# Third attention of a hybrid layer: values with tokens on the partitions, the divisor from a column of ones, normalized along the free axis and turned by transposes

## The chip, the cores and the metric

One core of one Trainium2 chip runs the whole program in one launch. The metric is the time of an execution on the device, in microseconds (us). The engines are named as in the profile: PE (TensorE, with PEld for its weight loads), DVE (VectorE), ACT (ScalarE), POOL (GpSimd) and SP (SyncE, which here starts the weight transfers).

## The reference

The program computes two layers of a hybrid block and then a second block, on 512 tokens with a model width of 1024, all in float32. Only the third branch of the two layers is touched by the change. It is an mLSTM with 4 heads of 128; the kernel computes it as a masked attention over all 512 tokens:

```python
s = einsum('bhtd,bhsd->bhts', q, k) * w_intra        # w_intra: decay of token s as seen from token t
num = einsum('bhts,bhse->bhte', s, v)
den = sum(s, axis=-1)
h = num / maximum(abs(den), exp(-m_row))             # divisor with a floor
# head_layer_norm, over the 128 values of a head
y = (h - mean(h)) * rsqrt(var(h) + 1e-6)
y_c = y * ml_norm_w * sigmoid(ml_o)
branch = y_c * silu(ml_z)                            # then w_branch, gates and w_out
```

With D the divisor of a token, the norm of num/D equals (num - mean(num))/sqrt(var(num) + eps*D^2); the changed kernel uses that form.

## The kernel before

All activations lie transposed: features on the 128 partitions, the 512 tokens along the free axis. Weights are streamed in chunks of 128x1024 float32 by SP into a ring of 4. Each chunk is split into a rounded high part by ACT (`Weights.round`, L120) and a low part by POOL (`Weights.rest`, L147), and a product of a 1024-deep layer takes 8 x 3 matmuls in fp32r over 512 columns (`Weights.product`, L171: high x high, low x high, high x low). Such a product is called dense below; a product of a branch (`gated_product`) is 4 x 3 matmuls. Matmuls that are not split run in true fp32, and the profile shows each of them as two records, one for each pass; a transpose is one record.

The order of the work is written out by hand, and every engine walks through the same list of results (`layer_groups`, L235). A result that takes a bank of the pair `proj` waits until the result two places before it in the list has been emptied (`Groups.open`, L289); six more banks, `att`, hold scores. `Groups.whole` waits for a result, `Groups.empty` signs its bank off, `Groups.moved` waits for that.

The stage of the change stands at the end of each layer's attentions (PE from L968, ACT from L1190, DVE from L1473, POOL from L1576). For each head h, PE computes the dense products `mlo` and `zc` (the two gates of the branch), two branch products `proj2h,0` and `proj2h+1,0` of the first branch, the scores of head h+2 (`ml_scores`, 4 matmuls of 512, 384, 256 and 128 columns) and these three:

- `den`: ones (128x128) as weights against the weighted scores `probs`, 4 matmuls of 512 to 128 columns. It gives the divisor's sum on all 128 partitions.
- `num`: the values `mv` as weights against the same `probs`.
- `var`: ones against the square of the result, one matmul of 512 columns, for the norm.

The values were centred before by DVE (`centre`, L1400, 8 times a layer), so `num` has mean zero over a head. DVE takes the maximum of |den| (ACT, Abs) and the floor, inverts it (L1482), multiplies `num` with it (L1484), and, after ACT has squared and PE has summed, inverts the root (L1490) and applies weight, root and both gates (L1491 to L1494). Before the divisor of the next head it empties the banks of the branch products (`first_gated`, L1457) and weighs the next head's scores (`ml_weigh`, L1463). The floor exp(-m) is one row a head; POOL writes it to memory and spreads it over the partitions by DMA (`spread_row`, L1544), as it does with the row for the decay. ACT computes the decay factors (`ml_decay`, L1175), and POOL sets the upper triangles to zero (L1580). The same stage follows again for the second layer. Behind it come the other branch products with their gates (`GATES`), in which the third branch is read from `zc`.

Of the kernel before, what the change touches and what calls it, by code (L numbers as in the profile page):

```python
# [7 lines left out]
F32 = mybir.dt.float32  # L8
F32R = mybir.dt.float32r
ALU = mybir.AluOpType  # L10
# [12 lines left out]
IDX_H = 4  # L23
TOPK = 128
# [3 lines left out]
TAKEN = -3e38  # L28
ALIVE = -2.5e38
# [200 lines left out]
AFTER_SUMS = [["gate00"], ["gate30"], ["gate40"], ["gate70"]]  # L230
GATES = [(0, 1), (1, 1), (0, 2), (1, 2)] + [(d, k) for d in range(2, KD) for k in (1, 2)]
# [3 lines left out]
def layer_groups(l):  # L235
# [22 lines left out]
    for i, (d, k) in enumerate(GATES):  # L258
        g += [(f"gate{d}{k}", "a")] + ([(f"var{ML_H - 1}", "a")] if i == 0 else []) + [(f"proj{d}{k}", "v")]
# [284 lines left out]
def hybrid_layers(nc, stack, S, A, scratch):  # L544
# [31 lines left out]
    dv_at, dv = here(nc), sb("dv", [P, TB, T])  # L576
# [13 lines left out]
    acol = sb("acol", [P, TB, ML_H])  # L590
# [33 lines left out]
    mq, mk, mv = dq, dk, dv  # L624
# [3 lines left out]
    hml, dn, hsq = bias[:, 0:T], bias[:, T:2 * T], misc[:]  # L628
    spread_mu, spread_floor = [idx[:, i, :] for i in range(2)], [idx[:, 2 + i, :] for i in range(2)]
# [27 lines left out]
    s_fl = [sem(f"s_floor_spread{i}", 32) for i in range(2)]  # L657
    s_decay = sem("s_decay", 4 * ML_H)
    s_masked = sem("s_masked", 3)
    s_csq = sem("s_csq", 1)  # L660
# [19 lines left out]
    s_centred = sem("s_centred", 8)  # L680
    s_silu = sem("s_silu", 2)
    s_gate0 = sem("s_gate0", 1)
# [4 lines left out]
    s_sq2 = sem("s_sq2", 4)  # L687
    s_mlz = sem("s_mlz", 4)
# [52 lines left out]
    def tensor(pe, l):  # L741
# [71 lines left out]
        for b in range(TB):  # L813
            tr = pe.transpose(out[:, b * ML_H:(b + 1) * ML_H], g_a[:, b * P:(b + 1) * P], ident[0:ML_H, 0:ML_H])
# [147 lines left out]
        def ml_var(h):  # L962

            out = G.open(pe, f"var{h}")
            pe.wait_ge(s_sq2.sem, s_sq2.base + h + 1)
            G.close(pe.matmul(out[:, :], ones, hsq, start=True, stop=True))

        for h in range(ML_H):  # L968
            dense(f"mlo{h}")
            if h >= 1:  # L970
                ml_var(h - 1)
            dense(f"zc{h}")
            if h == 0:
                ml_scores(0)
                ml_scores(1)
            gated_product(2 * h, 0)
            pe.wait_ge(s_ws.sem, s_ws.base + 3 * (h + 1))
            for n in ("den", "num"):
                out = G.open(pe, f"{n}{h}")
                if h == 0 and n == "num":  # L980
                    pe.wait_ge(s_centred.sem, s_centred.base + 2 * TB)
                for s in range(TB):
                    w = ones if n == "den" else mv[:, s, h * P:(h + 1) * P]
                    mm = pe.matmul(out[:, s * P:T], w, probs[:, h % 2, KOFF[s]:KOFF[s] + WK[s]],  # L984
                                   start=(s == 0), stop=(s == TB - 1), skip_group_check=True)
                G.close(mm)
            if h + 2 < ML_H:
                ml_scores(h + 2)
            gated_product(2 * h + 1, 0)

        for i, (d, k) in enumerate(GATES):
# [2222 lines left out]
```

## Time and profile before

| quantity | value |
|---|---|
| three timed runs | 2600.92, 2596.46, 2601.33 us; median 2600.92 |
| span of the profiled execution (first to last instruction) | 2593.4 us |
| the profiled execution's own time | no figure apart from its span; the timed runs lie 3.1 to 7.9 us above the span |
| PE busy | 2523.2 us (97%) |
| DVE, ACT, POOL busy | 1097.1, 1062.5, 1303.8 us (42, 41, 50%) |
| granted clock of TensorE | 0.993 of full speed |
| DMA | 227.23 MB, mean 88 GB/s |

The busy share of PE counts overlapping records once, and the duration of a matmul record holds its passage through the array as well. What a matmul costs in a stream is therefore read from the distance between the starts of two records and not from their durations. The stage of the change lies at 388 to 484 us in the first layer and at about 1073 to 1170 us in the second.

### The profile page before, as it was taken

Reading aid. Unit: us, or ns where it says so; the run is one execution under the profiler, and the core shown is the slowest. Engines: PE = TensorE matmul, PEld = TensorE weight load, DVE = VectorE, ACT = ScalarE, POOL = GpSimd, SP = SyncE. Lnnn points to the kernel's source line nnn. Section 1 sums busy time; section 2 is a strip of 40 time slices with the busy share of each in tenths; the row PEclk is TensorE's granted clock in tenths of the full one; section 3 lists DMA queues with packets and bytes.
Section 4 is the critical chain, followed back from the end, with each engine's and each line's share of the span. In section 5 each row is a group of like instructions: output and inputs, shape, how many; then the busy total and the mean of one; then the engine's idle time right before and its main releaser. Section 6 shows DMA issues by size and latency. Waiting matters only on the chain.

```text
span 2593.4 us, 32107 instructions
## 1 busy us (share of the span) xinstructions
PE 2523.2 (97%) x12502; PEld 2033.3 (78%) x12502; DVE 1097.1 (42%) x1893; ACT 1062.5 (41%) x1605; POOL 1303.8 (50%) x1790
## 2 busy tenths in 40 slices
PE   8999999999999999999999999999989899999998
PEld 6777887788777788778888888877967688888886
DVE  5855635522485563552243113098355422311101
ACT  5334667423433466732343323242355323322321
POOL 5444655555544465545555554574433255555453
PEclk9999999999999999999999999999999999999999
DMA  4222122222222212222232222331221122222222
GB/s 153 86 90 82 66 65 82 73 98 98 90 82 67 81 66 66 81 74 97 95 109 95 95 95 97 105 131 66 82 74 66 41 98 98 90 98 98 98 98 81
DMA packets 63698, 227.23 MB, mean 88 GB/s; under 512 B 7431, under 2 KB 8967, under 8 KB 63420
## 3 DMA queue, kind: packets, MB, share of 16 engines
q1 hardware_dynamic: 61276, 217.28, 24.9%
q0 software_dynamic: 2272, 7.90, 1.1%
q8 instruction: 100, 1.64, 0.3%
q14 instruction: 50, 0.41, 0.1%
HBM read 222.98 MB, written 4.01 MB: 88 GB/s over the span
## 4 chain that ended last, share of the span: by engine, by line
PE 89%; DVE 7%; ACT 3%; issue 1%; DMA 1%; DVEq 0%; SPq 0%; ACTq 0%
PE proj L180 75%; PE proj L877 1%; PE att L180 1%; PE att L914 1%; PE proj L984 1%; ACT b_logits L2371 1%; PE att L856 1%; PE att L900 1%; DVE h_low L530 1%; PE att L867 1%; PE att L958 1%; PE att L2029 1%; DVE hT L536 1%; DVE rstd L1490 1%; PE proj L763 0%
## 5 line engine op out<-in xcount | busy, mean ns | idle before, releaser
L157 POOL TENSOR_TENSOR weight_low<-ring,weight_high 128x256 fp32r<-128x256 f32 x1592 | 1229.2, 804 | 1145.7 <-ACT weight_high L127 1124.3
L180 PE MATMUL proj<-h_high,weight_high 128*128 128x512 f32 x2016 | 796.5, 395 | 17.9 <-ACT b_big L2214 13.0
L180 PE MATMUL proj<-h_high,weight_low 128*128 128x512 f32 x2016 | 786.0, 390 | 0.0
L180 PE MATMUL proj<-h_low,weight_high 128*128 128x512 f32 x2016 | 785.2, 389 | 0.0
L127 ACT ACTIVATE weight_high<-ring 128x1024 fp32r<-128x1024 f32 x393 | 413.9, 1054 | 410.4 <-PE proj L180 378.9
L180 PEld LDWEIGHTS proj<-h_high,weight_high 128*128 128x128 f32 x2016 | 378.8, 188 | 130.6 <-ACT b_big L2214 14.3
L180 PEld LDWEIGHTS proj<-h_low,weight_high 128*128 128x128 f32 x2016 | 378.9, 188 | 80.2
L180 PEld LDWEIGHTS proj<-h_high,weight_low 128*128 128x128 f32 x2016 | 379.3, 188 | 75.5 <-issue 0.2
L2562 DVE TENSOR_TENSOR b_big<-proj,b_big 128x512 f32<-128x512 f32 x42 | 29.0, 691 | 376.3 <-PE proj L180 376.3
L180 PE MATMUL proj<-b_act_high,weight_high 128*128 128x512 f32 x352 | 137.2, 390 | 0.0
L180 PE MATMUL proj<-b_act_high,weight_low 128*128 128x512 f32 x352 | 136.9, 389 | 0.0
L180 PE MATMUL proj<-b_act_low,weight_high 128*128 128x512 f32 x352 | 136.9, 389 | 0.0
L2214 ACT ACTIVATE b_big<-proj 128x512 f32<-128x512 f32 x58 | 34.6, 597 | 198.2 <-PE proj L180 198.1
L2583 DVE SCALAR_TENSOR_TENSOR xT<-proj,xT 128x512 f32<-128x512 f32 x16 | 11.1, 691 | 198.1 <-PE proj L180 198.1
L1507 DVE TENSOR_TENSOR turned<-proj,probs 128x512 f32<-128x512 f32 x32 | 22.1, 692 | 165.4 <-PE proj L180 165.3
L180 PE MATMUL proj<-weight_high,h_high 128*128 128x256 f32 x288 | 82.6, 287 | 2.1 <-ACT sv L1009 2.1
L180 PE MATMUL proj<-weight_low,h_high 128*128 128x256 f32 x288 | 81.5, 283 | 0.0
L180 PE MATMUL proj<-weight_high,h_low 128*128 128x256 f32 x288 | 81.5, 283 | 0.0
L180 PE MATMUL proj<-z_high,weight_high 128*128 128x512 f32 x192 | 76.2, 397 | 2.2 <-DVE turned L1507 2.2
L180 PEld LDWEIGHTS proj<-b_act_high,weight_high 128*128 128x128 f32 x352 | 66.1, 188 | 13.8 <-issue 0.2
L180 PEld LDWEIGHTS proj<-b_act_high,weight_low 128*128 128x128 f32 x352 | 66.1, 188 | 13.8
L180 PEld LDWEIGHTS proj<-b_act_low,weight_high 128*128 128x128 f32 x352 | 66.1, 188 | 13.7
(473 smaller groups left out, 3735.1 us busy)
## 6 DMA issues: line engine op xcount, KB each, us to landing
ring<-in_stream SPq DMA_DIRECT2D x398, 512.0 KB, 3.3
idx<-gate_rows POOLq DMA_DIRECT2D x16, 256.0 KB, 4.6
xT<-in_x SPq DMA_DIRECT2D x4, 512.0 KB, 6.5
out<-hT SPq DMA_DIRECT2D x4, 512.0 KB, 2.7
bias_rows<-bias_row SPq DMA_DIRECT2D x2, 512.0 KB
b_logits<-in_mem POOLq DMA_DIRECT2D x1, 1024.0 KB, 6.3
consts<-in_const SPq DMA_DIRECT2D x1, 832.0 KB, 10.3
bias_rows<-bias_row SPq DMA_DIRECT2D x1, 768.0 KB
```

The lines of the kernel that those rows point to most:

```text
L127: self.s_high.on(act.activation(self.high[:, c % HIGH, :], self.raw[:, c % self.slots, :], ACT.Copy))
L157: self.s_low.on(pool.tensor_tensor(self.low[:, c % self.slots, cols], self.raw[:, c % self.slots, cols], self.high[:, c % HIGH, cols], ALU ...
L180: mm = pe.matmul(out, a, b, start=(k == 0 and i == 0), stop=(k == n - 1 and i == 2))
L530: S.s_hl.on(dve.tensor_tensor(S.h_low[:, k, :], S.hT[:, k, :], S.h_high[:, k, :], ALU.subtract))
L536: S.s_h.on(dve.scalar_tensor_tensor(out[:, k, :], S.xT[:, k, :], weights[:, k:k + 1], S.att[5][:, :], ALU.mult, ALU.mult))
L856: mm = pe.matmul(att[2 * bank + hh][:, col:col + WQ[b]], dq[rows(hh), p, b * P:(b + 1) * P], dk[rows(hh), p, 0:WQ[b]], start=True, stop=True)
L867: tr = pe.transpose(att[2 * bank + hh][:, col + (b - s) * P:col + (b - s + 1) * P], probs[:, hh, OQ[b] + s * P:OQ[b] + (s + 1) * P], ident)
L877: mm = pe.matmul(out[rows(hh), s * P:T], v[:, s, h * HD:(h + 1) * HD], turned[:, hh, KOFF[s]:KOFF[s] + WK[s]], start=(s == 0), stop=(s == ...
L900: mm = pe.matmul(att[3 * hh + bank][:, col:col + WK[s]], sk[rows(hh), p, s * P:(s + 1) * P], sq_[rows(hh), p, s * P:T], start=(s != 3), st ...
L914: mm = pe.matmul(att[3 * hh + bank][:, col + (u - s) * P:col + WK[s]], signs[:, 0:P] if u == s else signs[:, P:2 * P], x, start=False, sto ...
L2214: G.empty(act.activation(out, bank[:, :] if src is None else src(bank), func, **kw), name)
L2562: G.empty(dve.tensor_tensor(big[:, i, :], bank[:, :], big[:, i, :], ALU.mult), f"{n}b{i}")
```

## The change

The scores stay as they are. The values are no longer centred; they are stored 130 apart for each head, with two columns of ones behind the 128 values. `num` now takes the 128x128 blocks of `probs` as weights and 129 columns of `mv` (128 values and a one) as the moving operand: 10 matmuls a head for the lower triangle of blocks, written to two of the head's three `att` banks (`s_num` signs it off). Tokens then stand on the partitions and the divisor's sum is column 128. `den` and `var` are gone, and with them their banks. DVE computes divisor, mean and variance in `ml_stats` with bn_stats and bn_aggr, ACT takes a root of 128x4 numbers (`ml_root`), DVE inverts it and applies mean and factor (`ml_apply`) into `by_token`, PE turns the result with four transposes a head into a `proj` bank (`y`), and DVE multiplies it with weight and gates (`ml_gated`; `ml_gate` forms the product of the gates beforehand). The floor is transposed along with the decay's column (`at`: 8 instead of 4 small transposes), and its exponential is taken of 128x16 numbers. The four DMAs a layer that spread the floor are gone. The order of the third stage is written out anew (`THIRD`), and with it the order on ACT, DVE and POOL. The sigmoid over `mixed` on ACT is split in two. The z_high parts of the third branch are taken at the first two of the later gates (two each) instead of all at the second.

```diff
+THIRD = [["mlo0", "zc0", "mls0", "mls1", "proj00", "num0", "proj10"],
+         ["mlo1", "y0", "mls2", "num1", "zc1", "proj20", "y1", "mls3", "proj30"],
+         ["num2", "mlo2", "zc2", "proj40", "y2", "proj50"],
+         ["num3", "mlo3", "zc3", "proj60", "y3", "proj70"]]
...
@@ -253,10 +259,9 @@
     for p in range(PAIRS_H):
         g += [(n, "a") for n in BEFORE_SUMS[p] + AFTER_SUMS[p]] + [(f"sb{p}", "v")]
     for h in range(ML_H):
-        g += [(f"mlo{h}", "a")] + ([(f"var{h - 1}", "a")] if h else []) + [(f"zc{h}", "a"), (f"proj{2 * h}0", "v")]
-        g += [(f"den{h}", "a"), (f"num{h}", "v"), (f"proj{2 * h + 1}0", "v")]
...
+        g += [(n, "v" if n[0] in "py" else "a") for n in THIRD[h] if n[:3] not in ("num", "mls")]
+    for d, k in GATES:
+        g += [(f"gate{d}{k}", "a"), (f"proj{d}{k}", "v")]
     g += [(f"out{d}", "v") for d in range(KD)]
     return g
...
@@ -621,12 +628,17 @@
     mix_low = rounded("mix_low", [P, KD, T], mix_at)
     mix_high2 = [rounded(f"mix_high{i}", [P, 4, T], at) for i, at in enumerate((sq_at, sv_at))]
     mix_high = [mix_high2[k // 4][:, k % 4, :] for k in range(KD)]
-    mq, mk, mv = dq, dk, dv
+    dv = dv_all[:, 0:TB * T].rearrange("p (a b) -> p a b", a=TB)
+    mv = dv_all[:].rearrange("p (a b c) -> p a b c", a=TB, b=ML_H)
+    mq, mk = dq, dk
     ckv = idx[:, 3, :]
     gate = probs[:].rearrange("p a b -> p (a b)")[:, 0:3 * T].rearrange("p (a b) -> p a b", a=3)
     part = turned[:].rearrange("p a b -> p (a b)")[:, 0:2 * T].rearrange("p (a b) -> p a b", a=2)
-    hml, dn, hsq = bias[:, 0:T], bias[:, T:2 * T], misc[:]
-    spread_mu, spread_floor = [idx[:, i, :] for i in range(2)], [idx[:, 2 + i, :] for i in range(2)]
+    by_token = [bias[:, i * T:(i + 1) * T].rearrange("p (a b) -> p a b", a=TB) for i in range(2)]
+    spread_mu = [idx[:, i, :] for i in range(2)]
+    stats = small[:, 0:6 * TB].rearrange("p (a b) -> p a b", a=TB)
+    moments = small[:, 24:24 + 2 * TB].rearrange("p (a b) -> p a b", a=TB)
+    s_den, s_square, s_dev, s_factor = (small[:, 32 + TB * i:32 + TB * (i + 1)] for i in range(4))
     csq = dk[:, 0, :]
     tflat = turned[:].rearrange("p a b -> p (a b)")
...
@@ -810,8 +823,10 @@
         dense("zb1")
         out = G.open(pe, "at")
         pe.wait_ge(s_gates.sem, s_gates.base + 1)
-        for b in range(TB):
-            tr = pe.transpose(out[:, b * ML_H:(b + 1) * ML_H], g_a[:, b * P:(b + 1) * P], ident[0:ML_H, 0:ML_H])
+        for i, rows_ in enumerate((g_a, g_m)):
+            for b in range(TB):
+                at = (i * TB + b) * ML_H
+                tr = pe.transpose(out[:, at:at + ML_H], rows_[:, b * P:(b + 1) * P], ident[0:ML_H, 0:ML_H])
         G.close(tr)
         dense("zb2")
         dense("zb3")
...
@@ -952,46 +967,50 @@
                 pe.wait_ge(s_a_exp.sem, s_a_exp.base + 3 * HEADS)
                 pe.wait_ge(s_silu.sem, s_silu.base + 2)
             else:
-                pe.wait_ge(s_ws.sem, s_ws.base + 3 * (h - 1))
+                pe.wait_ge(s_by_token.sem, s_by_token.base + h - 1)
             for s in range(TB):
                 bank, col = KPLACE[s]
                 mm = pe.matmul(att[3 * (h % 2) + bank][:, col:col + WK[s]], mk[:, h, s * P:(s + 1) * P], mq[:, h, s * P:T],
                                start=True, stop=True)
             s_K.on(mm)
-        def ml_var(h):
-
...
+        def ml_values(h):
+            pe.wait_ge(s_ws.sem, s_ws.base + 3 * (h + 1))
+            if h == 0:
+                pe.wait_ge(s_ones.sem, s_ones.base + 1)
+                G.moved(pe, "mlv7")
+            for b in range(TB):
+                out, col = att[3 * (h % 2) + b // 2], VALUE * (b % 2)
+                for s in range(b + 1):
+                    at = KOFF[s] + (b - s) * P
+                    mm = pe.matmul(out[:, col:col + ML_D + 1], probs[:, h % 2, at:at + P], mv[:, s, h, 0:ML_D + 1],
+                                   start=(s == 0), stop=(s == b), skip_group_check=True)
+            s_num.on(mm)
+        def ml_turn(h):
+            out = G.open(pe, f"y{h}")
+            pe.wait_ge(s_by_token.sem, s_by_token.base + h + 1)
+            for b in range(TB):
+                tr = pe.transpose(out[:, b * P:(b + 1) * P], by_token[h % 2][:, b, :], ident)
+            G.close(tr)
         for h in range(ML_H):
-            dense(f"mlo{h}")
-            if h >= 1:
...
+            for n in THIRD[h]:
+                if n[:3] == "mls":
+                    ml_scores(int(n[3:]))
+                elif n[:3] == "num":
+                    ml_values(int(n[3:]))
+                elif n[0] == "y":
+                    ml_turn(int(n[1:]))
+                elif n[:4] == "proj":
+                    gated_product(int(n[4]), 0)
+                else:
+                    dense(n)
+        for d, k in GATES:
             dense(f"gate{d}{k}")
-            if i == 0:
-                ml_var(ML_H - 1)
             gated_product(d, k)
         for d in range(KD):
             out = G.open(pe, f"out{d}")
...
         def fill(names):
             for n in names:
                 if n[:3] in ("sbv", "mlv"):
                     i = int(n[3:])
-                    move(n, (sv if n[0] == "s" else mv)[:, i % TB, (i // TB) * HALF:(i // TB + 1) * HALF],
-                         rows_=slice(0, HALF))
+                    if n[0] == "s":
+                        move(n, sv[:, i % TB, (i // TB) * HALF:(i // TB + 1) * HALF], rows_=slice(0, HALF))
+                        continue
+                    W.round(act, n)
+                    bank = G.whole(act, n)[:, 0:HALF].rearrange("p (a b) -> p a b", a=2)
+                    G.empty(act.activation(mv[:, i % TB, 2 * (i // TB):2 * (i // TB) + 2, 0:ML_D], bank, ACT.Copy), n)
                 elif n[:2] == "ml":
                     h = int(n[3:]) + (4 if n[2] == "k" else 0)
                     if h == 0:
...
@@ -1183,45 +1206,50 @@
                 s_decay.on(act.activation(turned[:, h % 2, KOFF[s]:KOFF[s] + WK[s]], spread_mu[h % 2][:, s * P:T], ACT.Exp,
                                           bias=acol[:, s, h:h + 1]))
-        def ml_var(h):
-
-            move(f"var{h}", rstd[:], ACT.Sqrt, scale=1.0 / ML_D, bias=S.eps)
+        def ml_root(h):
+            act.wait_ge(s_dev2.sem, s_dev2.base + h + 1)
+            s_root.on(act.activation(s_dev, s_dev, ACT.Sqrt))
         ml_decay(0)
+        ml_decay(1)
         move("mlo0", mlo[:, 0, :], ACT.Sigmoid)
         G.moved(act, f"dsa{PAIRS_H - 1}")
         for j in range(4):
             s_zh.on(act.activation(z_high[0][:, j, :], za[:, j, :], ACT.Copy))
         settle(act, s_a)
-        s_gate0.on(act.activation(mixed, mixed, ACT.Sigmoid))
-        for h in range(ML_H):
...
+        s_gate0.on(act.activation(mixed[:, 0:2, :], mixed[:, 0:2, :], ACT.Sigmoid))
+        s_gate0.on(act.activation(mixed[:, 2:KD, :], mixed[:, 2:KD, :], ACT.Sigmoid))
+        move("zc0", zc[:, 0, :], ACT.Silu)
+        W.round(act, "proj00")
+        ml_root(0)
+        W.round(act, "proj10")
+        move("mlo1", mlo[:, 1, :], ACT.Sigmoid)
+        ml_decay(2)
+        ml_root(1)
+        move("zc1", zc[:, 1, :], ACT.Silu)
+        W.round(act, "proj20")
+        ml_decay(3)
+        W.round(act, "proj30")
+        act.wait_ge(s_K.sem, s_K.base + ML_H)
+        G.moved(act, f"sb{PAIRS_H - 1}")
+        for j in range(4):
+            s_zh.on(act.activation(z_high[1][:, j, :], zb[:, j, :], ACT.Copy))
+        for h in (2, 3):
+            ml_root(h)
+            move(f"mlo{h}", mlo[:, h, :], ACT.Sigmoid)
             move(f"zc{h}", zc[:, h, :], ACT.Silu)
             W.round(act, f"proj{2 * h}0")
-            if h + 1 < ML_H:
-                ml_decay(h + 1)
-            move(f"den{h}", dn, ACT.Abs)
             W.round(act, f"proj{2 * h + 1}0")
-            G.moved(act, f"num{h}")
-            s_sq2.on(act.activation(hsq, hml, ACT.Square))
...
+        act.wait_ge(s_num.sem, s_num.base + ML_H)
         for n, (d, k) in enumerate(GATES):
             if n >= 3:
                 G.moved(act, "proj{}{}".format(*GATES[n - 3]))
             move(f"gate{d}{k}", gate[:, n % 3, :], ACT.Sigmoid)
-            if n == 0:
-                ml_var(ML_H - 1)
             W.round(act, f"proj{d}{k}")
-            if (d, k) == (1, 1):
-                act.wait_ge(s_mlz.sem, s_mlz.base + ML_H)
-                for j in range(4):
+            if n < 2:
+                for j in range(2 * n, 2 * n + 2):
+                    G.moved(act, f"y{j}")
                     s_zh.on(act.activation(z_high[2][:, j, :], zc[:, j, :], ACT.Copy))
             if n >= 3 and GATES[n - 1][1] == 2:
                 e = GATES[n - 1][0]
...
@@ -1437,6 +1456,9 @@
         for p in range(PAIRS_H):
             if p == 0:
                 gated(f"dsa{PAIRS_H - 1}", PAIRS_H - 1, za)
+                s_ones.on(dve.memset(mv[:, :, :, ML_D:VALUE], 1.0))
+                dve.wait_ge(s_floor.sem, s_floor.base + 1)
+                link(dve.tensor_scalar(fcol, fcol, FLOOR_TOP, None, ALU.min))
             else:
                 gated(f"sb{p - 1}", p - 1, zb)
             soft_sum(p, 0)
...
         def first_gated(d):
             bank = G.whole(dve, f"proj{d}0")
-            if d == 0:
-                dve.wait_ge(s_gate0.sem, s_gate0.base + 1)
+            dve.wait_ge(s_gate0.sem, s_gate0.base + (1 if d < 2 else 2))
             G.empty(dve.tensor_tensor(mixed[:, d, :], bank[:, :], mixed[:, d, :], ALU.mult), f"proj{d}0")
         def ml_weigh(h):
...
@@ -1465,34 +1484,87 @@
             dve.wait_ge(s_w8m.sem, s_w8m.base + TB * (h + 1))
             dve.wait_ge(s_K.sem, s_K.base + h + 1)
             if h >= 2:
-                G.whole(dve, f"num{h - 2}")
+                dve.wait_ge(s_num.sem, s_num.base + h - 1)
             for bank, n, at in BANKS:
                 s_ws.on(dve.scalar_tensor_tensor(probs[:, h % 2, at:at + n], att[3 * (h % 2) + bank][:, 0:n], ML_D ** -0.5,
                                                  turned[:, h % 2, at:at + n], ALU.mult, ALU.mult))
+        def ml_stats(h):
+            dve.wait_ge(s_num.sem, s_num.base + h + 1)
+            banks = [att[3 * (h % 2) + i][:, 0:2 * VALUE].rearrange("p (a b) -> p a b", a=2) for i in range(2)]
+            for i in range(2):
+                s_vc.on(dve.tensor_tensor(s_den[:, 2 * i:2 * i + 2], banks[i][:, :, ML_D], fcol[:, 2 * i:2 * i + 2, h],
+                                          ALU.max))
+            for b in range(TB):
+                s_vc.on(dve.bn_stats(stats[:, b, :], banks[b // 2][:, b % 2, 0:ML_D]))
+            settle(dve, s_vc)
+            for i in range(2):
+                s_vc.on(dve.scalar_tensor_tensor(s_den[:, 2 * i:2 * i + 2], banks[i][:, :, ML_D], -1.0,
+                                                 s_den[:, 2 * i:2 * i + 2], ALU.mult, ALU.max))
+            settle(dve, s_vc)
+            s_vc.on(dve.tensor_tensor(s_square, s_den, s_den, ALU.mult))
+            for b in range(TB):
+                s_vc.on(dve.bn_aggr(moments[:, b, :], stats[:, b, :]))
+            settle(dve, s_vc)
+            s_dev2.on(dve.scalar_tensor_tensor(s_dev, s_square, EPS, moments[:, :, 1], ALU.mult, ALU.add))
+        def ml_apply(h):
+            dve.wait_ge(s_root.sem, s_root.base + h + 1)
+            link(dve.reciprocal(s_factor, s_dev))
+            if h >= 2:
+                G.whole(dve, f"y{h - 2}")
+            for b in range(TB):
+                x = att[3 * (h % 2) + b // 2][:, VALUE * (b % 2):VALUE * (b % 2) + ML_D]
+                ins = dve.tensor_scalar(by_token[h % 2][:, b, :], x, moments[:, b, 0:1], s_factor[:, b:b + 1],
+                                        ALU.subtract, ALU.mult)
+                if b < TB - 1:
+                    s_vc.on(ins)
+            s_by_token.on(ins)
+        def ml_gate(h):
+            G.moved(dve, f"mlo{h}")
+            G.moved(dve, f"zc{h}")
+            link(dve.tensor_tensor(zc[:, h, :], zc[:, h, :], mlo[:, h, :], ALU.mult))
+        def ml_gated(h):
+            bank = G.whole(dve, f"y{h}")
+            ins = dve.scalar_tensor_tensor(zc[:, h, :], bank[:, :], vecs[:, 41 + h:42 + h], zc[:, h, :], ALU.mult, ALU.mult)
+            G.empty(ins, f"y{h}")
         branch_low(0)
         ml_weigh(0)
-        for h in range(ML_H):
-            if h == 2:
...
+        first_gated(0)
+        ml_weigh(1)
+        ml_stats(0)
+        ml_apply(0)
+        first_gated(1)
+        ml_gate(0)
+        ml_gated(0)
+        ml_stats(1)
+        ml_weigh(2)
+        ml_apply(1)
+        first_gated(2)
+        ml_gate(1)
+        ml_gated(1)
+        first_gated(3)
+        ml_weigh(3)
+        ml_stats(2)
+        branch_low(1)
+        ml_apply(2)
+        first_gated(4)
+        ml_gate(2)
+        ml_gated(2)
+        first_gated(5)
+        ml_stats(3)
+        ml_apply(3)
+        first_gated(6)
+        ml_gate(3)
+        ml_gated(3)
+        first_gated(7)
         def mixed_low(d):
             dve.wait_ge(s_mh.sem, s_mh.base + d + 1)
...
@@ -1570,20 +1642,14 @@
                 for s in range(TB):
                     s_am.on(triangle(turned[:, hh, KOFF[s]:KOFF[s] + P], ALU.is_gt, 1, 0.0))
             W.rest(pool, AFTER_SUMS[p][-1])
-        pool.wait_ge(s_tri.sem, s_tri.base + HEADS)
-        spread_row(1, 0)
-        spread_row(1, 1)
         for h in range(ML_H):
-            W.rest(pool, f"zc{h - 1}" if h else "gate70")
+            W.rest(pool, ("gate70", "gate70", "mlo1", "zc1")[h])
             pool.wait_ge(s_decay.sem, s_decay.base + TB * (h + 1))
             for s in range(TB):
                 s_w8m.on(triangle(turned[:, h % 2, KOFF[s]:KOFF[s] + P], ALU.is_ge, 1, 0.0))
             if h + 2 < ML_H:
-                spread_row(0, h + 2)
-            if 1 <= h < 3:
...
+                spread_row(h + 2)
+        W.rest(pool, "proj30")
         W.rest(pool, f"out{KD - 1}")
     def loads(sp, l):
```

## Rows read from the trace of the kernel before

**Rows 1.** The page: busy time by engine, and the chain that ended last.

```profile
PE 2523.2 (97%) x12502; PEld 2033.3 (78%) x12502; DVE 1097.1 (42%) x1893; ACT 1062.5 (41%) x1605; POOL 1303.8 (50%) x1790
...
PE 89%; DVE 7%; ACT 3%; issue 1%; DMA 1%; DVEq 0%; SPq 0%; ACTq 0%
```

**Rows 2.** Waits of the tensor engine: engine, line, total us, times, longest.

```profile
PE proj L984 <- DVE raw L1461: 6.3, 2, 3.1
...
PE proj L180 <- DVE turned L1507: 2.2, 2, 1.1
...
PE proj L180 <- DVE bias L1484: 1.0, 2, 0.6
```

**Rows 3.** Timeline of PE in third attention, layer 0: start, duration, engine, line.

```profile
403.69 2.40 PE L984 MATMUL proj<-probs,consts_all 128*128 128x512 f32 x8
...
425.13 0.39 PE L180 MATMUL proj<-z_high,weight_high 128*128 128x512 f32 x1
...
427.85 2.32 PE L984 MATMUL proj<-probs,consts_all 128*128 128x512 f32 x8
430.00 2.32 PE L984 MATMUL proj<-probs,dv 128*128 128x512 f32 x8
432.16 2.32 PE L958 MATMUL att<-dq,dk 128*128 128x512 f32 x8
```

**Rows 4.** Timeline of PE around the variance product of head 0.

```profile
418.71 1.02 PE L966 MATMUL proj<-misc,consts_all 128*128 128x512 f32 x2
419.56 0.50 PE L180 MATMUL proj<-h_high,weight_high 128*128 128x512 f32 x1
419.89 0.40 PE L180 MATMUL proj<-h_high,weight_low 128*128 128x512 f32 x1
```

**Rows 5.** Timeline of PE around twenty transposes of the first attention.

```profile
194.89 2.35 PE L867 MATMUL att<-consts_all,probs 128*128 128x128 f32 x20
...
197.31 0.39 PE L180 MATMUL proj<-h_high,weight_low 128*128 128x512 f32 x1
```

**Rows 6.** Timeline of PE: four true fp32 products of 128 columns, eight passes.

```profile
21.67 1.05 PE L503 MATMUL att<-consts_all,scal 128*128 128x128 f32 x8
...
22.80 0.39 PE L180 MATMUL att<-lead_high,weight_low 128*128 128x512 f32 x1
```

**Rows 7.** Line 503 grouped: weight loads, ns min/median/max.

```profile
L503 PEld LDWEIGHTS att<-consts_all,scal x48: 187/190/338, 21.4 to 2584.3; 128*128 128x128 f32 x48
```

**Rows 8.** Timeline of PE and DVE at the longest wait of head 2.

```profile
452.40 4.06 DVE L1455 TENSOR_TENSOR z_low<-zb,z_high 128x512 fp32r<-128x512 f32 x4
...
457.12 2.42 PE L984 MATMUL proj<-probs,dv 128*128 128x512 f32 x8 [3.15 <-DVE raw L1461]
```

**Rows 9.** Timeline of ACT at the head of the stage.

```profile
390.32 1.92 ACT L1183 ACTIVATE turned<-idx,acol 128x512 f32<-128x512 f32 x4
...
397.09 3.60 ACT L1196 ACTIVATE raw<-raw 128x4096 f32<-128x4096 f32 x1
...
402.95 0.60 ACT L1009 ACTIVATE sk<-proj 128x512 f32<-128x512 f32 x1
```

**Rows 10.** Timeline of DVE: small operations, and the weighting of scores.

```profile
256.18 0.17 DVE L1364 TENSOR_SCALAR small<-small 128x4 f32<-128x4 f32 x1
...
257.09 1.28 DVE L1373 TENSOR_SCALAR probs<-probs,small 128x128 f32<-128x128 f32 x4
...
322.92 0.42 DVE L1405 TENSOR_REDUCE small<-dv 128x2 f32<-128x256 f32 x1
```

**Rows 11.** Timeline of DVE in third attention.

```profile
399.01 1.62 DVE L1470 SCALAR_TENSOR_TENSOR probs<-att,turned 128x512 f32<-128x512 f32 x3
...
408.96 3.35 DVE L1482 RECIPROCAL bias<-bias 128x512 f32<-128x512 f32 x1
```

**Rows 12.** Timeline of PE at the gate transposes.

```profile
111.87 0.41 PE L814 MATMUL proj<-consts_all,idx 4*128 4x4 f32 x4
112.62 0.50 PE L180 MATMUL proj<-h_high,weight_high 128*128 128x512 f32 x1 [0.35 <-ACT zb L1009]
```

More of the change, by code:

```diff
@@ L23 @@
 IDX_H = 4
+VALUE = ML_D + 2
 TOPK = 128
@@ L28 @@
 TAKEN = -3e38
+FLOOR_TOP = 1e18
 ALIVE = -2.5e38
@@ L575, in hybrid_layers @@
     dk_at, dk = here(nc), sb("dk", [P, 4, T])
-    dv_at, dv = here(nc), sb("dv", [P, TB, T])
+    dv_at, dv_all = here(nc), sb("dv", [P, TB * ML_H * VALUE])
+    sb("line_up2", [P, LINE_UP])
     sq_at, sq_ = here(nc), sb("sq_", [P, 4, T])
@@ L656, in hybrid_layers @@
     s_mu = [sem(f"s_mu_spread{i}", 32) for i in range(2)]
-    s_fl = [sem(f"s_floor_spread{i}", 32) for i in range(2)]
     s_decay = sem("s_decay", 4 * ML_H)
     s_masked = sem("s_masked", 3)
+    s_ones = sem("s_ones", 1)
+    s_num = sem("s_num", ML_H)
+    s_dev2 = sem("s_dev_square", ML_H)
+    s_root = sem("s_dev_root", ML_H)
+    s_by_token = sem("s_by_token", ML_H)
     s_csq = sem("s_csq", 1)
@@ L960, in ml_scores @@
             s_K.on(mm)
-        def ml_var(h):
-            out = G.open(pe, f"var{h}")
-            pe.wait_ge(s_sq2.sem, s_sq2.base + h + 1)
-            G.close(pe.matmul(out[:, :], ones, hsq, start=True, stop=True))
-        for h in range(ML_H):
-            dense(f"mlo{h}")
-            if h >= 1:
[L971 to L989, printed above, removed]
@@ L1084, in scalar @@
         act.preload_act_table_set("natural_log_exp_and_others")
-        act.wait_ge(s_gates.sem, s_gates.base + 1)
-        s_floor.on(act.activation(g_m, g_m, ACT.Exp))
+        G.moved(act, "at")
+        s_floor.on(act.activation(fcol, fcol, ACT.Exp))
         def fill(names):
@@ L1218, in scalar @@
             move(f"gate{d}{k}", gate[:, n % 3, :], ACT.Sigmoid)
-            if n == 0:
-                ml_var(ML_H - 1)
             W.round(act, f"proj{d}{k}")
-            if (d, k) == (1, 1):
-                act.wait_ge(s_mlz.sem, s_mlz.base + ML_H)
-                for j in range(4):
+            if n < 2:
+                for j in range(2 * n, 2 * n + 2):
+                    G.moved(act, f"y{j}")
                     s_zh.on(act.activation(z_high[2][:, j, :], zc[:, j, :], ACT.Copy))
@@ L1447, in vector @@
                 conv(h)
-            for i in ([], range(4), [], range(4, 8))[p]:
-                centre(i)
         gated(f"sb{PAIRS_H - 1}", PAIRS_H - 1, zb)
@@ L1473, in vector @@
+        def ml_gate(h):
[6 more added lines that the diff above has]
+            G.empty(ins, f"y{h}")
         branch_low(0)
         ml_weigh(0)
-        for h in range(ML_H):
-            if h == 2:
-                branch_low(1)
-            first_gated(2 * h)
-            G.moved(dve, f"den{h}")
-            dve.wait_ge(s_fl[h % 2].sem, s_fl[h % 2].base + 16 * (h // 2 + 1))
-            link(dve.tensor_tensor(dn, dn, spread_floor[h % 2], ALU.max))
-            link(dve.reciprocal(dn, dn))
-            bank = G.whole(dve, f"num{h}")
-            G.empty(dve.tensor_tensor(hml, bank[:, :], dn, ALU.mult), f"num{h}")
-            first_gated(2 * h + 1)
-            if h + 1 < ML_H:
-                ml_weigh(h + 1)
-            settle(dve, s_v)
-            G.moved(dve, f"var{h}")
-            link(dve.reciprocal(rstd[:], rstd[:]))
-            link(dve.scalar_tensor_tensor(hml, hml, vecs[:, 41 + h:42 + h], rstd[:], ALU.mult, ALU.mult))
-            link(dve.tensor_tensor(hml, hml, mlo[:, h, :], ALU.mult))
-            G.moved(dve, f"zc{h}")
-            s_mlz.on(dve.tensor_tensor(zc[:, h, :], zc[:, h, :], hml, ALU.mult))
-            settle(dve, s_mlz)
@@ L1555, in gpsimd @@
                 pool.wait_ge(s_rows_out.sem, s_rows_out.base + 16)
[L1556 to L1557 removed]
+                G.moved(pool, "at")
+                spread_row(0)
+                spread_row(1)
         for p in range(PAIRS_H):
```

46 lines of the change are left out of this document (10 added, 36 removed).

## The prediction

> **What bounds the kernel now.** I read the page first, then the waits of PE, then timelines of the stage that changes. On the page the reader is to see that PE is busy 97% of the span and carries 89% of the chain that ended last [rows 1]; nothing else is near half of either. So an edit is worth what it takes from PE's stream or from PE's waits, and work on DVE, ACT and POOL is worth nothing until it makes PE wait. The table of waits [rows 2] holds three lines that belong to the changed stage: `num` waiting for a bank that DVE frees with a branch product (6.3 us in two waits, one a layer), a product waiting for the gate multiplication (2.2), one waiting for the bank of `num` (1.0). The timeline says why the longest exists: DVE spends 4.06 us on the low parts of the second branch, behind the norm of head 1, and only then empties the bank; PE stands still for 3.15 us [rows 8].
>
> **How the prices are read.** Twelve split matmuls of 512 columns run from 425.13 to 427.85, that is 0.227 us each [rows 3]. Behind a run of true fp32 the first of them takes 0.33 instead (419.56 to 419.89) [rows 4]; I call the 0.10 an edge.
>
> **What goes from PE.** `den` runs from 427.85 to 430.00: 2.15 us. `num` after it takes 2.16 (to 432.16) [rows 3]. `var` with its edge: 419.89 - 418.71 - 0.23 = 0.95 [rows 4]. Removed per head 2.15 + 0.95 = 3.10.
>
> **What comes to PE.** Four transposes a head. Twenty take 197.31 - 194.89 - 0.23 = 2.19 with an edge, so 0.105 each [rows 5]; four are 0.42, with an edge 0.52.
>
> **What changes shape.** `num` was 1280 columns under 4 weight loads; it becomes 10 x 129 = 1290 columns under 10, each in two passes, so 20 loads of 128 columns with only 129 columns to hide one. The trace has no such group with real scores as weights. The old `num` gives 2.16 / 2560 = 0.84 ns a column and pass, so 2.18 us. The nearest row in shape are four fp32 products of 128 x 128: 22.80 - 21.67 - 0.23 - 0.10 = 0.80 for eight passes, 0.10 each, 2.0 for twenty [rows 6]. From above: a load's own record lasts 0.190 us [rows 7]; if that set the pace, twenty passes would be 3.8. I take 2.18: rows 6 have the same loads at almost the same width, at a pace of 0.10. That is +0.02 a head.
>
> Per head 3.10 - 0.52 - 0.02 = 2.56 us, and eight heads (4 in each of 2 layers) give 20.5. The new order also puts y0 next to scores and `num1`, and y1 next to scores, so there are 8 runs of fp32 in a layer where there were 9: 0.2 more over two layers. Sum of PE work: 20.7 us.
>
> The Trainium skill (TensorE: Matmul & The Clock Gate, Part 3: Packing small matmuls) speaks against this: it says that a weight load overlaps a running matmul only where the row groups differ, and all matmuls here use all rows. The transposes of rows 5 load 128 columns for each 128 that they stream and keep 0.105 us, so this trace does not agree. What the rule would make of the time is the third rival below.
>
> **What goes of the waits.** In the new order DVE does the low parts of the second branch behind the statistics of head 2, with two dense products and one branch product of PE still ahead of the next thing needed, and `num` takes no bank of the pair. The 3.35 us reciprocals of 512 columns [rows 11] shrink to 4 columns (0.17, as the small operation in rows 10), so the gates at the end of the stage find their banks empty. I count all three lines: 6.3 + 2.2 + 1.0 = 9.5 us. Their bounds are 0 (another wait stands there) and 9.5.
>
> **What is late next.** I walked PE through the new order with a dense product of 425.13 - 419.56 = 5.57, a branch product of 2.72 and scores of about 2.1 [rows 3, 4]. DVE's chain for one head is ten operations on at most 4 columns at 0.17, four bn_stats that I price by the 256-wide reduction at 0.42, the inverse at 0.17 and four applications at 1.28 [rows 10]: 1.7 + 1.7 + 0.2 + 1.3 = 4.9, and some 0.2 for ACT's root between. The trace shows no bn_stats; from below they are 0.17 each, which takes 1 us off.
> - Head 0: `num0` ends at 403.69 + 2.18 = 405.9, DVE is done at 411.0. PE has a branch and a dense product to do and asks for it at 414.2. Slack 3.
> - Head 1: PE does a dense and a branch product after `num1`, 8.3 us; DVE has the chain and the weighting of head 2, 1.62 [rows 11], between: 6.7. Slack 1.6, the tightest.
> - Head 2: 13.9 us of PE against the chain, the weighting of head 3 and 4.06 of low parts: 10.8. Slack 3. Head 3: 13.9 against 5.1.
> Behind the waiting turn stands all of PE, so each microsecond beyond the slack is lost in full.
>
> At the head of the stage ACT now does the decay of head 1 before emptying `mlo0`: 1.92 us, and the sigmoid over `mixed` (3.60) in two pieces, some 0.2 more [rows 9]. Everything behind slides by 2.1: the bank of `zc0` is empty at 402.95 + 0.60 + 2.1 = 405.65, and PE asks for it at 405.87, after `num0`. That is a margin of 0.2, so between nothing and 0.5 us a layer; I take 0.1. The weighting of head 0 ends at 399.01 + 1.62 = 400.63 [rows 11] and slides to 402.7, a microsecond before `num0` wants it at 403.69 [rows 3].
>
> **At nothing.** Four more small transposes: the four of before take 0.41, and behind them PE waits 0.35 for a bank [rows 12], which covers them but for 0.1. The centring is DVE work in a stage where DVE holds nobody up; the ones and the clamp of the floor go into an idle microsecond there. The floor's DMAs and POOL's issue of them free POOL a little, which is off the path. Copying the values to a stride of 130 moves as many elements as before.
>
> **Sum.** 20.7 + 9.5 - 0.2 = 30.0 us. On the profiled span 2593.4 becomes 2563.4. The span lies 7.5 below the median of the timed runs (2600.92), and I keep that distance: 2570.9.
>
> **The rivals.**
> 1. *The sums hold*, waits gone, no new one above 1 us: 2567 to 2575. 68%. Another 5% for less than 2567, if the block products run at the 0.10 of rows 6 (8 x 0.18 = 1.4 us) and the median before was high; the lowest run was 4.5 below it.
> 2. *The loads set the pace of the block products*: 20 x (0.190 - 0.108) = 1.6 a head, 13 us in all, 2584. For it: 188 to 190 ns is what every load's record shows. Against: rows 5 and 6, whose passes follow each other faster. 8%.
> 3. *The loads hide under nothing*: 20 x 0.190 = 3.8 a head for `num` and 0.76 for the turn, 36.5 in all, 2607. Against it the same rows. 2%. It is what the rule of the Trainium skill (TensorE: Matmul & The Clock Gate, Part 3) would do here.
> 4. *DVE's chain takes the place of the bank waits.* Place: y1 first, then y0 and y2. With 4 us more on each head the stalls are 2.4 + 1 + 1 a layer, 9 in both: 2580. The scalars are many small dependent operations that read PSUM, which speaks for it; the durations of 0.17 speak against. 14% for 2576 to 2590.
> 5. *The same chain, so long that the kernel is slower.* The gain of 30 is lost when both layers wait 15 each: 4x - (3 + 1.6 + 3 + 8.8) = 15, x = 7.9 us more on every head, the chain 13 instead of 5. Even bn_stats at the pace of the reciprocal (6.5 ns a column, rows 11) add only 1.6. 3% for 2606 or more.
>
> **The numbers.** The likeliest case gives 2570.9. The range 2564 to 2585 takes in the first two cases and most of the fourth, the reach of the block products' price (2.0 to 3.8) and of the waits (0 to 9.5 would be 2580). A measurement of this kernel can tell 0.2% (5 us) from no change. Faster by more than that: everything but the third and fifth case and a thin part of the fourth, 95%; within it 1%; slower 4%.
>
> **What would show it.** Right: no records of `var` and `den`; twenty records of 129 columns following each other at 0.105 to 0.11 us; four transposes a head in 0.42; the three lines of rows 2 gone; PE's busy time down by about 20. Wrong: PE standing before a transpose for `by_token` (case 4), or the weight loads of `num` end to end (case 2, 3). The forecast falls if the starts of the block products lie 0.19 apart, or if any wait of the new stage exceeds 2 us.

## The result: 37 us faster, 7 us more than predicted

Four executions of each kernel have medians of 2561.78 us (changed) and 2599.02 us (before): 37.2 us less, ratio 0.9856 with a 95% interval of 0.9841 to 0.9872. The forecast was 2570.9, the range 2564 to 2585: the direction was right, the gain of 30.0 too small, and the time lies 2.2 us below the range.

The page of the changed kernel, its head and its chain, beside [rows 1]: PE is 24.1 us less busy and carries 2 points more of the chain.

```profile
span 2560.3 us, 32269 instructions
...
PE 2499.1 (98%) x12558; PEld 2030.3 (79%) x12558; DVE 1036.3 (40%) x1977; ACT 1043.9 (41%) x1587; POOL 1290.1 (50%) x1782
...
PE 91%; DVE 5%; ACT 3%; DMA 1%; issue 1%; SPq 0%; DVEq 0%; ACTq 0%
```

The waits of PE. The three lines of [rows 2] are gone; one of 0.35 us a time has come, at the branch products behind the turns of heads 2 and 3.

```profile
PE proj L182 <- DVE raw L1480: 1.4, 4, 0.3
```

The timeline of PE: the block products of head 0 and what follows, then turn, scores and block products of head 1. It answers to [rows 3 to 5].

```profile
405.65 2.40 PE L987 MATMUL att<-dv,probs 128*128 128x129 f32 x20
407.80 0.47 PE L182 MATMUL proj<-z_high,weight_high 128*128 128x512 f32 x1
...
416.09 0.60 PE L996 MATMUL proj<-consts_all,bias 128*128 128x128 f32 x4
416.53 2.32 PE L973 MATMUL att<-dq,dk 128*128 128x512 f32 x8
418.69 2.40 PE L987 MATMUL att<-dv,probs 128*128 128x129 f32 x20
420.84 0.47 PE L182 MATMUL proj<-h_high,weight_high 128*128 128x512 f32 x1
```

Twenty passes take 2.15 us from start to start (I had 2.18), the turn 0.44. DVE's chain for head 0, beside [rows 10]:

```profile
408.08 0.23 DVE L1497 TENSOR_TENSOR small<-att,acol 128x2 f32<-128x2 f32 x2
408.23 0.88 DVE L1500 BATCH_NORM_STATS2 small<-att 128x6 f32<-128x128 f32 x4
...
409.82 0.37 DVE L1508 BATCH_NORM_AGGREGATE small<-small 128x2 f32<-128x6 f32 x4
...
410.86 0.18 DVE L1515 RECIPROCAL small<-small 128x4 f32<-128x4 f32 x1 [0.27 <-ACT small L1212]
411.07 1.37 DVE L1520 TENSOR_SCALAR bias<-att,small 128x128 f32<-128x128 f32 x4
```

From 408.08 to 412.44 it takes 4.4 us where I had 5.1, and its result lies there 3.6 us before PE turns it at 416.09.

The stage as a whole, from the first product on the scores of head 0 to the first product behind the last changed wait (the third of the later gates), by the starts of these rows. The kernel before (den of head 0; beyond [rows 3]), layer 0 and layer 1:

```profile
503.66 0.39 PE L180 MATMUL proj<-h_high,weight_high 128*128 128x512 f32 x1
...
1051.41 2.39 PE L984 MATMUL proj<-probs,consts_all 128*128 128x512 f32 x8
...
1152.82 0.39 PE L180 MATMUL proj<-h_high,weight_high 128*128 128x512 f32 x1
```

The changed kernel, the same places (the first one is 405.65 above):

```profile
490.14 0.39 PE L182 MATMUL proj<-h_high,weight_high 128*128 128x512 f32 x1
...
1037.87 2.40 PE L987 MATMUL att<-dv,probs 128*128 128x129 f32 x20
...
1122.37 0.39 PE L182 MATMUL proj<-h_high,weight_high 128*128 128x512 f32 x1
```

Before: 503.66 - 403.69 = 99.97 and 1152.82 - 1051.41 = 101.41. After: 84.49 and 84.50. So the stage gives 15.48 and 16.91 us. The difference between the layers is 1.4 us, and the stretches say where it lies. The kernel before, 4 us of PE behind the wait of head 2, in layer 0 and layer 1. The columns are length, PE busy (records), granted clock as a share of full speed, DMA share and GB/s:

```profile
457.00:461.00 4.00, 3.88 (x15) 1.00 0.00 0
1105.00:1109.00 4.00, 4.00 (x11) 0.65 0.00 0
```

In layer 1 the clock stands at its lower level, 1.2 GHz instead of 2.4, behind the wait. At full clock the change is thus worth 2 x 15.5 = 31.0 us, against the 30.0 of my sum. What the experiments had to find is the rest of the 37.

### The profile page after: what moved, and what is told of

Its sections match the earlier page's. It is cut to its first block, busy times and chain, and to the rows that moved or that the text cites. A ratio compares the mean times of both kernels' runs of the same rounds, so it can differ in the third digit from the quotient of the medians.

```text
span 2560.3 us, 32269 instructions
## 1 busy us (share of the span) xinstructions
PE 2499.1 (98%) x12558; PEld 2030.3 (79%) x12558; DVE 1036.3 (40%) x1977; ACT 1043.9 (41%) x1587; POOL 1290.1 (50%) x1782
## 4 chain that ended last, share of the span: by engine, by line
PE 91%; DVE 5%; ACT 3%; DMA 1%; issue 1%; SPq 0%; DVEq 0%; ACTq 0%
PE proj L182 77%; PE att L182 1%; PE proj L892 1%; PE att L929 1%; ACT b_logits L2437 1%; PE att L871 1%; PE att L915 1%; PE att L987 1%; DVE h_low L535 1%; PE att L882 1%; PE att L973 1%; PE att L2095 1%; DVE hT L541 1%; PE proj L776 0%; PE att L2230 0%
```

## The experiments

Theory A: a wait of PE costs what the trace records. Theory B: the changed kernel is granted more clock as such. Theory C, formed on the repeated trace of the kernel before (e1): a long wait also drops the granted clock to half for some microseconds behind it. Times are medians, of 9 to 15 executions for the kernel before (2597.3 to 2597.7) and of only 4 to 6 for the others. "Over the changed kernel" is against 2561.75, its median in e2 and e10.

How far a median can be trusted, the traces say. Behind the stage of layer 1 the program is the same in every version, and yet it takes from 1433.2 us (e5) to 1443.9 us (e9) there. So single executions can lie up to 11 us apart for reasons outside the changed stage, and the distances between rows of the stage tell more than a median of four.

**e1, the kernel before against itself.** No edit.

> The kernel before, once more against itself, to see how far single executions of one program lie apart and whether its granted clock differs from that of the changed kernel. Theory A (the trace of the change holds: 31.0 us from PE's stream and waits, the rest of the 37.2 us between the medians is chance in the granted clock): ratio 1.000 within 0.002, executions spread over 5 us or more, and their clocks over 0.002. Rival B (the changed kernel is granted more clock as such): the clocks of this one lie below those of the changed kernel on the same chip by 0.002 or more in the mean.

Ratio 0.9999 (0.999 to 1.0007); 2592.01 to 2600.55. The eleven clocks are 0.990 to 0.993, 0.9919 in the mean; four of the changed kernel 0.992 to 0.996, 0.9933 in the mean (e2). That is 0.0013 apart where B asked for 0.002; over 45 executions of the kernel before and 12 of the changed one it is 0.002. So the changed kernel does run at a little more clock, and the trace names a place where the kernel before loses some: the same two waits, in layer 0 and layer 1.

```profile
457.00:461.00 4.00, 3.60 (x6) 0.57 0.00 0
...
1106.00:1110.00 4.00, 3.36 (x5) 0.50 0.02 4
```

`num` of head 2 in layer 0 takes 3.81 us from start to start (457.40 to 461.21), against 2.18 in the first trace (457.12 to 459.30).

```profile
457.40 4.05 PE L984 MATMUL proj<-probs,dv 128*128 128x512 f32 x8 [3.15 <-DVE raw L1461]
461.21 0.48 PE L180 MATMUL proj<-z_high,weight_high 128*128 128x512 f32 x1
```

**e2 and e10, the changed kernel again.** No edit.

> The changed kernel, once more. Theory A: on more executions the difference to the kernel before comes towards the 31 us of the traces, 29 to 34 us, ratio 0.987 to 0.989. Rival B (a clock gain comes on top): it stays at 36 to 38 us, ratio 0.9855 to 0.986, and the mean clock is above that of the kernel before by 0.002.

> The changed kernel a third time, to narrow the difference between the medians. Theory C says: 31.0 us of PE work and waits as the traces give it, and 1.5 to 4.4 us of half clock behind the waits of head 2 (as in the two traces of the kernel before), so 32.5 to 35.5 us faster than the kernel before. Theory A: 31.

2561.73 and 2561.75, ratios 0.9860 (0.9843 to 0.9877) and 0.9858 (0.9843 to 0.9872): 35.8 us both times. Theory A's 31 lies outside both intervals (31.9 and 33.2 us at the least), and C's upper end of 35.5 is inside them, just short of the value.

The traces agree with C more closely. The four spans of the kernel before (the first, e1, e11, e12) have a mean of 2595.6 us, the three of the changed kernel (the first, e2, e10) one of 2561.4: 34.2 us. The two stages alone, read as above in the same seven traces, differ by 34.4 us.

**e3, the order alone.** On the kernel before:

```diff
         for h in range(ML_H):
-            if h == 2:
-                branch_low(1)
             first_gated(2 * h)
...
                 ml_weigh(h + 1)
+            if h == 2:
+                branch_low(1)
             settle(dve, s_v)
```

> The kernel before with one edit: DVE does the low parts of the second branch in the idle time ahead of the norm of head 2 and not before its first branch product. Nothing else of the change is in it. My term for the longest wait says that both waits of 3.15 us go and nothing takes their place: 6.3 us faster, ratio 0.9976. Rival: num waits for the bank anyway, since DVE's chain for the divisor (0.7 + 3.35 + 0.7 us) stands between the branch product and the emptying of num; then under 3 us are won.

9.7 us faster (ratio 0.9965, 0.9953 to 0.9978, which is 5.7 to 12.2 us), where 6.3 were expected. Yet its trace gives back less than 6.3: a small wait has come in place of each long one, and from the first `den` (404.23, 1049.43) to the third later gate (501.68, 1146.84) the stage is 2.5 us a layer shorter than the 99.97. So 5.0 us are waits, and 4.7 by the medians are not; 5.0 alone lies just outside the interval. With the 3.5 us that the half clock costs the kernel before (e11 and e12 below) it would be 8.5. The lines are those of layer 0:

```profile
PE proj L180 <- DVE bias L1482: 1.2, 2, 0.6
PE proj L180 <- DVE turned L1507: 1.1, 1, 1.1
```

**e9, half of that edit.** Two of the four low parts stay in place (`branch_low(1, (0, 1))`), two move (`branch_low(1, (2, 3))`).

> The kernel before with half of the edit of e3: two of the four low parts stay ahead of DVE's first branch product of head 2, two go behind. The wait of num at head 2 should shrink from 3.15 to about 1.1 us (two operations of 1.0 us less), so 4 us of waiting go in two layers, of which e3's trace gave back 1.2 in new small waits. Theory A (waits cost themselves): 3 to 4 us faster than the kernel before. Theory C (a wait of over 2 us also drops the granted clock to half behind it, one of 1.1 does not): the 4 us or so of clock come back too, 7 to 9 us faster, nearly as much as e3 (9.8), and the profile shows full clock behind the wait of head 2.

6.3 us faster (0.9971, 0.9959 to 0.9983). The wait is 1.33 us and the clock behind it is full in both layers; the stage is 1.9 us a layer shorter. So 3.8 are waiting and 2.5 come on top. A's 3 to 4 lies just outside the interval (4.4 to 10.7 us), C's 7 to 9 inside it, though above the value. The wait and the 8 us from its end on, in layer 0:

```profile
455.17 2.42 PE L984 MATMUL proj<-probs,dv 128*128 128x512 f32 x8 [1.33 <-DVE raw L1461]
...
455.00:459.00 4.00, 3.83 (x15) 1.00 0.00 0
459.00:463.00 4.00, 4.00 (x19) 1.00 0.34 124
```

**e5 and e6, waits put into the changed kernel.** In `ml_stats`, e6 (e5 has the second one on 256 columns):

```diff
             settle(dve, s_vc)
+            for _ in range(2):
+                link(dve.reciprocal(rstd[:], rstd[:]))
             s_dev2.on(dve.scalar_tensor_tensor(s_dev, s_square, EPS, moments[:, :, 1], ALU.mult, ALU.add))
```

> The changed kernel with idle DVE work in each head's statistics: the reciprocal of a 512-column tile nobody reads, and of half of it, 3.35 + 1.7 = 5.05 us a head (it changes nothing else). In the trace of the changed kernel the bank that the turn of head 0 needs is free 3.0 us before the turn and the token tile of head 1 is done 3.0 us before its turn; heads 2 and 3 have 7 and 9.6 us. So PE should wait 2.0 us at each of two places a layer, 8 us in all. Theory A (a wait costs itself): 8 us over the changed kernel. Theory C (a long wait also lets the granted clock fall to half behind it, as in the repeated trace of the kernel before, and short ones do not): also 8 if 2 us is short, up to 18 if it is long.

> The same with two whole reciprocals, 6.7 us a head. Waits by the same slack: 3.7 us at head 0 and 3.7 at head 1, none at heads 2 and 3, in both layers 15 us. Theory A (a wait costs itself): 15 us over the changed kernel, and no stretch at half clock in the stage. Theory C (the clock falls behind a wait of over 3 us): 1.5 to 3 us more for each of the four waits, 21 to 27 us over the changed kernel, with the clock at about half in some 5 us behind each wait.

e5: 9.6 us over the changed kernel; its waits are 1.8 and 2.2 us in each layer, 8.0 in all, as the slack read in the changed kernel's trace had said. Behind the 1.8 the clock stays (first stretch), behind the 2.2 it falls (second stretch), 1.7 us lost each time. By the trace the two losses and the waits make 11.4 us; the median of five executions cannot tell that from A's 8.

```profile
416.17 0.66 PE L996 MATMUL proj<-consts_all,bias 128*128 128x128 f32 x4 [1.82 <-DVE raw L1480]
...
431.58 0.63 PE L996 MATMUL proj<-consts_all,bias 128*128 128x128 f32 x4 [2.16 <-ACT sk L1028]
...
416.00:420.00 4.00, 3.83 (x23) 1.00 0.29 108
432.00:436.00 4.00, 4.00 (x12) 0.61 0.00 0
```

e6: 26.0 us over. The waits at heads 0 and 1 are 3.4 and 3.8 (I had 3.7 each); a wait of 1.0 at heads 2 and 3 I had not seen, for a bank that ACT empties behind its root. Together 19.6 a run, 18.2 more than the 1.4 of the changed kernel. The other 8 us are the four long waits: half clock behind every one. From each of the four turns to the next block products the trace has 1.7, 3.0, 2.6 and 1.5 us more than the trace of the changed kernel has at the same places, 8.8 in all. A's 15 is far below the 26.0, C's 21 to 27 holds it.

```profile
418.00:422.00 4.00, 3.79 (x10) 0.64 0.02 4
437.00:441.00 4.00, 4.00 (x9) 0.50 0.00 0
1066.00:1070.00 4.00, 4.00 (x9) 0.50 0.00 0
1086.00:1090.00 4.00, 4.00 (x14) 0.74 0.00 0
```

**e7, the removed work put back without its waits.** Behind each head's `num`:

```diff
+            for s in range(TB):
+                mm = pe.matmul(att[3 * (h % 2) + 2][:, s * P:T], ones, probs[:, h % 2, KOFF[s]:KOFF[s] + WK[s]],
+                               start=(s == 0), stop=(s == TB - 1), skip_group_check=True)
+            mm = pe.matmul(att[3 * (h % 2) + 2][:, :], ones, mq[:, h, :], start=True, stop=True)
             s_num.on(mm)
```

> The changed kernel with the removed PE work put back as dead work and without its waits: behind each head's num four products of ones and the weighted scores (512 to 128 columns) and one of 512 columns, into the head's unused third bank. Terms of my sum: 2.15 + 0.85 = 3.0 us a head, 24.0 us in all, since it costs no edge. Theory C (the clock fell because of the wait of head 2): 24 us over the changed kernel and no half clock in the stage. Rival D (the clock falls with the amount of true fp32 work): 27 to 30 us, with half clock in the stage though PE nowhere waits there.

26.0 us over by the medians, of five and four executions; this cannot be told from 24, nor from D's 27. The trace can: the stage to the first later gate is 80.17 us (403.79 to 483.96) against 68.17 (405.65 to 473.82), 12.0 a layer, 24.0 in all, the term as expected. The clock is full through both stages, so rival D (the amount of fp32 work) falls:

```profile
403.00:484.00 81.00, 80.31 (x386) 1.00 0.18 59
1048.00:1128.00 80.00, 79.31 (x381) 1.00 0.19 60
```

**e8, half of the columns.** `num` streams columns 64 to 128 of each head (values and one) instead of 0 to 128, so it leaves half of the values out.

> The changed kernel with half of the values left out of num: each of its matmuls streams 65 columns (64 values and the ones) instead of 129 under the same 128-column weight loads. If columns set the pace, a pass takes 0.055 us instead of 0.108, 1.07 us a head, 8.5 us faster than the changed kernel. If the weight loads set a floor near the present pace of 0.107 us, nothing is gained: within 1 us. Between: a floor at some other pace, to be read from the distance of the records.

2562.85 us, 1.1 over the changed kernel: nothing gained. Twenty passes of 65 columns keep 2.15 us, to the hundredth what 129 columns take:

```profile
403.42 2.34 PE L987 MATMUL att<-dv,probs 128*128 128x65 f32 x20
405.57 0.47 PE L182 MATMUL proj<-z_high,weight_high 128*128 128x512 f32 x1
```

So there is a floor of 0.107 us under such a pass, and 129 columns happen to fill it. What did not change is the load of 128 columns ahead of each pass. That the load makes the floor is my reading; another fixed cost of a pass was not tried apart from it.

**e4, the turns ahead of both branch products**, to win the 1.4 us of new waits: `"zc2", "y2", "proj40", "proj50"` in `THIRD`, the same for head 3, and DVE's order to match.

> The changed kernel with the turns of heads 2 and 3 put ahead of both branch products instead of between them, and DVE's order to match. In the trace of the changed kernel each of these branch products waits 0.35 us for a bank behind the short turn, four times in all. If the bank is the cause, the four waits go: 1.4 us faster than the changed kernel in its profiled span at equal clock. Rival: the turn now waits for its token tile (DVE is done 7 and 10 us before the old place of the turns, 2.7 us of which are given up), so no new wait is expected; if one shows, the gain is less than 1.4 or negative.

2562.32 us, not to be told from the changed kernel. The expected 1.4 us did not come: the stage to the first later gate is 67.99 us against 68.20 in e2, 0.4 us in all. The turn's successor now waits 0.25 us for the bank of `zc`, which ACT has only begun to empty. No version beats the changed kernel measurably.

```profile
445.37 0.60 PE L996 MATMUL proj<-consts_all,bias 128*128 128x128 f32 x4
446.22 0.50 PE L182 MATMUL proj<-z_high,weight_high 128*128 128x512 f32 x1 [0.25 <-ACT sk L1028]
```

**e11 and e12, two more traces of the kernel before.**

> One more trace of the kernel before, to count how often half clock stands behind the wait of head 2. Theory C: in at least one of the two layers the products behind the 3.15 us wait run at half clock for 3.4 or 6.8 us and cost 1.4 to 2.9 us. Theory A: none, as in layer 0 of the first trace.

> The same once more: four traces of the kernel before then show eight such waits. Theory C: a mean loss of 1.5 to 2.5 us behind each wait, 3 to 5 us in an execution, which is what e3 won beyond its waits (9.8 - 5.1 = 4.7 us).

The two executions took 2596.28 and 2597.34 us. From the end of the wait to the variance product of head 2 the first trace needs 467.59 - 457.12 = 10.47 us at full clock in layer 0. The other seven of eight need more, by 1.5 (first trace, layer 1), 1.6 and 2.9 (e1), 2.9 and 1.7 (e11), 1.7 and 1.6 (e12). Mean over the eight 1.7 us a wait, 3.5 an execution. All eight waits are recorded at 3.15 us, so the length alone does not say how much is lost. One of the two heaviest, e11 in layer 0:

```profile
457.00:461.00 4.00, 3.45 (x5) 0.50 0.00 0
461.00:465.00 4.00, 4.00 (x14) 0.68 0.00 0
```

## Why the prediction fell short

- **PE's work (20.7 us predicted).** Held. The block products cost what I took, the turn 0.44 of 0.42 to 0.52, and e7 gives the removed work back at 24.0; less eight turns that is 20.5. The price of the block products was right partly by luck: I took it from their columns, and e8 shows that half of the columns take as long, 0.107 us a pass. It is not the 0.190 of the load's own record either, so rivals 2 and 3 fall.
- **The waits (9.5 us predicted): the step that failed.** I priced each wait at its recorded length. At full clock that is a little low: the wait of 1.08 us makes its place 1.39 longer (493.97 to 500.80 where a dense product takes 5.44), that of 3.15 makes it 3.32. The turns' four new waits of 0.35 us take about as much away again, and the stage comes to 31.0 against my 30.0; I did not split that 1.0 us further. The larger part is the clock behind the 3.15 us waits: seven of eight are followed by half clock, 3.5 us an execution. e5 and e6 produce the loss where there was none, e7 has the work without the waits and without the loss, and in e3 and e9 it is gone with the long wait. By their medians e3 won 4.7 beyond its waits and e9 2.5, each give or take some 3 us. That the clock falls behind the long waits, and what it costs there, is shown. Why it did not fall behind one of the eight is open. The trace that I had showed one of these drops (0.65 in layer 1, above); I read the clock only as 0.993 over the span.
- **What was to be late next.** Nothing was; the chain of 4.4 us left about 3 us at heads 0 and 1. For head 0 that is the slack of the prediction, for head 1 it had 1.6. e5 hit its 8.0 us of waits with the slack of the changed kernel's trace, not with mine. The turns of e5 and e6 waited for banks (L1480, L1028), not for `by_token`, which I had named as the sign. Rivals 4 and 5 did not occur. The margin of `proj10` held without a wait. The dead spot behind the short turns (4 x 0.35) I had not seen.
- **From span to median (7.5 us predicted): the second step that failed, by about as much.** I set the profiled span 7.5 us below its median. In every execution since, time and span lie 1.7 to 1.9 apart, so the profiled one took about 2595.1 while I started from a median of 2600.92; over 45 executions the kernel before has 2597.5. That is 3.4 us of the 9.1 by which 2570.9 was too high; the clock is 3.5 and the stage 1.0. With either of the two larger ones right, the time would have been inside the range.
- **Open.** 31.0 and 3.5 make 34.5 us; the repeated medians differ by 35.8. The intervals of e2 and e10 reach down to 31.9 and 33.2, so the 1.3 us are within what four executions of the changed kernel leave open, and I did not separate them.

## What to carry to other kernels

A wait of the tensor engine is not worth its length alone: look at the granted clock of the few microseconds behind it, in windows and not over the span. In this stage waits of 2.2 to 3.8 us cost 1.5 to 3 us more in 13 of 14 cases. Shortening such a wait can be worth nearly as much as removing it: 1.33 us instead of 3.15 brought 6.3 us, no long wait at all 9.7, though the intervals of the two overlap. Before believing a span, lay executions side by side: four of the changed kernel lay 10.7 us apart (e2).

## What the runs showed of the hardware

- At waits of 2.2 us and more (13 of 14: the traces of the kernel before, e5, e6) the clock fell to its lower level, for 3.4 or 6.8 us. It fell between 1.2 us before the wait's end and 1.3 us behind it, in executions of the same program at different moments. Behind waits of 1.8 us or less in the same stage it stayed at the upper one (e5, e9). Nothing between was tried.
- True fp32 products of 128x128 weights follow each other every 0.107 us a pass whether they stream 65 or 129 columns (e8), while the record of each load lasts 0.19.
- bn_stats over 128 columns in PSUM: four in 0.88 us; bn_aggr: four in 0.37.
